# Dummy products, smaller first weight loads and later constants at the start of a two-block decoder kernel

## The reference

```python
def rms_norm(x, g):
    xf = x.astype(jnp.float32)
    y = xf * lax.rsqrt(jnp.mean(xf * xf, axis=-1, keepdims=True) + RMS_EPS)
    return (y * g.astype(jnp.float32)).astype(x.dtype)

def first_block(...):
    h = rms_norm(x, norm1_g[l])
    proj = h @ w_in[l]                     # 2048 wide, in blocks of 512 columns
    qa, ka, va, ra, ga, qb, kb, vb = jnp.split(proj, split_points, axis=-1)
...
    qb = rms_norm(qb.reshape(Bsz, S, DIL_HEADS, DIL_DH), q_norm_g[l])
    kb = rms_norm(kb.reshape(Bsz, S, DIL_HEADS, DIL_DH), k_norm_g[l])
...
    x = x + mix @ w_out[l]
    h2 = rms_norm(x, norm2_g[l])
    x = x + (jax.nn.silu(h2 @ w_gate[l]) * (h2 @ w_up[l])) @ w_down[l]
```

## Time and profile before

| | |
|---|---|
| time, median of 3 runs | 1984.41 us (1983.95 to 1984.6) |
| the profiled execution | 1984.17 us, of which 1982.4 are its span |
| TensorE busy | 1963.4 us (99%) |
| VectorE, ScalarE, GpSimd busy | 1098.0 us (55%), 940.4 us (47%), 108.1 us (5%) |
| DMA | 352.74 MB, mean 178 GB/s |

### The profile page before, as it was taken

One profiled execution on the slowest core, in us unless ns is written; L12 is line 12 of the kernel. 1 busy time (PEld: TensorE's weight loads), 2 busy tenths in 40 slices (PEclk: granted clock), 3 DMA queues, 4 the chain that ended last, 5 costly groups with the idle time before them and its releaser, 6 DMA issues.

```text
span 1982.4 us, 22700 instructions
## 1 busy us (share of the span) xinstructions
PE 1963.4 (99%) x9062; PEld 1609.4 (81%) x9062; DVE 1098.0 (55%) x1330; ACT 940.4 (47%) x1230; POOL 108.1 (5%) x326
## 2 busy tenths in 40 slices
PE   8999999999999999999999999999999999999998
PEld 6788887788888888888888888888888887777787
DVE  4556455664445544455445565545556566666664
ACT  5445454554444344443444554444444454655652
POOL 1111000200000000000000010001100011100000
PEclk9999999999999999999999999999999999999999
DMA  7566564566665666666666566665566655444445
GB/s 232 179 192 170 151 176 153 159 180 183 196 190 189 195 191 185 190 190 192 195 189 190 184 186 193 189 191 171 167 184 190 191 180 176 132 138 140 138 132 164
DMA packets 182441, 352.74 MB, mean 178 GB/s; under 512 B 11136, under 2 KB 11952, under 8 KB 182336
## 3 DMA queue, kind: packets, MB, share of 16 engines
q1 hardware_dynamic: 181520, 349.18, 58.6%
q0 software_dynamic: 816, 2.11, 0.7%
HBM read 349.14 MB, written 2.11 MB: 177 GB/s over the span
## 4 chain that ended last, share of the span: by engine, by line
PE 92%; DVE 2%; POOL 2%; issue 1%; ACT 1%; DMA 0%; SPq 0%; DVEq 0%; POOLq 0%; ACTq 0%
PE g L773 29%; PE g L775 28%; PE g L774 28%; PE m L738 3%; PE m L841 1%; DVE wl L1201 1%; PE m L840 1%; DVE TW L1201 1%; DVE st L1210 1%; POOL st L1565 1%; ACT TW L961 1%; PE m L847 1%; ACT wh L964 1%; POOL st L1563 0%; POOL st L1569 0%
## 5 line engine op out<-in xcount | busy, mean ns | idle before, releaser
L1201 DVE TENSOR_TENSOR wl<-raw,wh 128x1024 fp32r<-128x1024 f32 x657 | 801.4, 1223 | 772.3 <-ACT wh L964 772.1
L964 ACT ACTIVATE wh<-raw 128x1024 fp32r<-128x1024 f32 x657 | 694.7, 1059 | 853.1 <-PE g L775 850.0
L773 PE MATMUL g<-wh,xh 128*128 128x512 f32 x1888 | 749.5, 397 | 2.6 <-DVE wl L1201 2.6
L775 PE MATMUL g<-wh,xl 128*128 128x512 f32 x1888 | 737.1, 390 | 0.0
L774 PE MATMUL g<-wl,xh 128*128 128x512 f32 x1888 | 736.1, 390 | 0.0
L773 PEld LDWEIGHTS g<-wh,xh 128*128 128x128 f32 x1888 | 355.1, 188 | 82.7 <-issue 8.5
L775 PEld LDWEIGHTS g<-wh,xl 128*128 128x128 f32 x1888 | 354.9, 188 | 75.4
L774 PEld LDWEIGHTS g<-wl,xh 128*128 128x128 f32 x1888 | 355.4, 188 | 70.1
L773 PE MATMUL g<-wh,mh 128*128 128x512 f32 x736 | 291.8, 396 | 0.0
L775 PE MATMUL g<-wh,ml 128*128 128x512 f32 x736 | 287.1, 390 | 0.0
L774 PE MATMUL g<-wl,mh 128*128 128x512 f32 x736 | 286.9, 390 | 0.0
(11 more groups left out here) (127 smaller groups left out, 872.5 us busy)
## 6 DMA issues: line engine op xcount, KB each, us to landing
raw<-in_ev_w_in SPq DMA_DIRECT2D x128, 512.0 KB, 3.7
raw<-in_w_in SPq DMA_DIRECT2D x96, 512.0 KB, 3.9
raw<-in_w_gate SPq DMA_DIRECT2D x88, 512.0 KB, 4.4
raw<-in_w_up SPq DMA_DIRECT2D x88, 512.0 KB, 3.7
raw<-in_w_down SPq DMA_DIRECT2D x88, 512.0 KB, 3.8
raw<-in_od_w_in SPq DMA_DIRECT2D x72, 512.0 KB, 3.7
raw<-in_w_out SPq DMA_DIRECT2D x32, 512.0 KB, 3.9
raw<-in_ev_w_out SPq DMA_DIRECT2D x32, 512.0 KB, 4.8
```

The costliest lines, as they stand in the source:

```text
L773: e.matmul(o, hi[:, kt, c], h, start=first, stop=False)
L775: last = e.matmul(o, lo[:, kt, c], h, start=False, stop=end)
L964: return e.activation(o, i, AF.Copy, scale=scale)
L1201: return e.tensor_tensor(o, a, b, op)
```

## The change

Five things change. (1) The first block's first unit is cut in two units of one row block each, so the first two loads are of 256 KB and that block has nine units in place of eight; all later units have a number that is one higher. (2) These two loads are issued by ScalarE as its first instructions; SP issues the others, x parts 0 and 1 first. (3) A new step `warm`: VectorE fills 384 columns of TE with 0.5, and TensorE makes four float32 products of 256 columns from it, into a PSUM bank that is overwritten later. (4) The steps of the start stand in another order: `cut 0` before the first `xturn`, and all eight `xturn` before the first `sq`. (5) The small constants are loaded after the load of unit 12.

```diff
@@ all_units
-        for a in range(0, len(b.kts), per):
-            units.append(Unit(len(units), b, b.kts[a:a + per], a == 0, a + per >= len(b.kts)))
+        starts = [0, 1] if b.i == 0 else []
+        starts += range(per if starts else 0, len(b.kts), per)
+        for a, z in zip(starts, starts[1:] + [len(b.kts)]):
+            units.append(Unit(len(units), b, b.kts[a:z], a == 0, z == len(b.kts)))
@@ Plan.lay
         self.lanes["post"].append(self.first_acts())
+        say("warm")
+        say("cut", 0)
         self.step()
-        say("cut", 0)
         self.step()
         say("cut", 1)
...
-            if b.n == 512:
+            if len(un.kts) == 2:
                 say("mul", u, 1)
@@ Plan.first_acts
         for kt in range(0, KT, 2):
             self.say("xturn", "X0", kt)
-            if kt % 4 == 2:
-                self.say("sq", 0, kt // 4)
+            yield
+        for j in range(4):
+            self.say("sq", 0, j)
             yield
         self.say("norm", 0)
@@ tensor
+                elif kind == "warm":
+                    on.wait_ge(s_warm, 1)
+                    for i in range(4):
+                        e.matmul(MB[2][:, 0:256], TE[:, 0:128], TE[:, 128:384], start=True, stop=True)
@@ scalar
             te_free = (s_act_step, 0)
+            weights(e, 0).then_inc(s_raw[0], 16)
+            weights(e, 1).then_inc(s_raw[1], 16)
@@ vector
+                elif kind == "warm":
+                    e.memset(TE[:, 0:384], 0.5).then_inc(s_warm, 1)
@@ sync
             e.dma_start(small[:, 0:nid], t["small"][:, 0:nid]).then_inc(s_id, 16)
-            load_x(0)
-            load(0)
-            load_x(1)
-            load(1)
-            load_x(2)
-            e.dma_start(small[:, nid:], t["small"][:, nid:]).then_inc(s_small, 16)
+            tokens(e, 0).then_inc(s_x[0], 16)
+            tokens(e, 1).then_inc(s_x[1], 16)
             load(2)
-            load_x(3)
+            tokens(e, 2).then_inc(s_x[2], 16)
             load(3)
-            load_x(4)
+            tokens(e, 3).then_inc(s_x[3], 16)
             load(4)
+            tokens(e, 4).then_inc(s_x[4], 16)
             load(5)
...
                 if kind == "cut" and a[0] >= LEAD and a[0] + NR < N:
                     load(a[0] + NR)
+                    if a[0] == 8:
+                        e.dma_start(small[:, nid:], t["small"][:, nid:]).then_inc(s_small, 16)
```

More of the change, by code:

```diff
@@ L553, in program @@
         s_pv, s_ob_act, s_ob_dve = sem("s_pv"), sem("s_ob_act"), sem("s_ob_dve")
-        s_split = sem("s_split")
+        s_split, s_warm = sem("s_split"), sem("s_warm")
         s_sq, s_nsum = sem("s_sq"), sem("s_nsum")
@@ L731, in aw_free, with weights, tokens @@
             return full(*before[-1]) if before else (s_bank, 0)
+        def weights(e, u):
+            un = units[u]
+            b, m = un.block, len(un.kts)
+            w = t[b.w]
+            if b.col is None:
+                src = w.rearrange("p (t n) -> p t n", n=b.n)
+            else:
+                r0 = b.row + 128 * un.kts[0]
+                src = w[r0:r0 + 128 * m, b.col:b.col + b.n].rearrange("(t p) n -> p t n", p=128)
+            return e.dma_start(raw[:, u % NR, 0:m * b.n].rearrange("p (t n) -> p t n", t=m), src)
+        def tokens(e, i):
+            a, z = XPARTS[i]
+            return e.dma_start(x[:, :, a:z], t["x"].rearrange("(t p) d -> p t d", p=128)[:, :, a:z])
         def tensor(e):
@@ L739, in four @@
                 return last
-            on.wait_ge(s_id, 16)
             for p in plan.order:
@@ L775, in tensor @@
                             last = e.matmul(o, lo[:, kt, c], h, start=False, stop=end)
-                    if half == 1:
+                    if half == len(un.kts) - 1:
                         last.then_inc(s_mul, 1)
+                elif kind == "warm":
+                    on.wait_ge(s_warm, 1)
+                    for i in range(4):
+                        e.matmul(MB[2][:, 0:256], TE[:, 0:128], TE[:, 128:384], start=True, stop=True)
                 elif kind == "xturn":
@@ L780, in tensor @@
                     if stage == 0:
+                        on.wait_ge(s_id, 16)
                         on.wait_ge(s_x[[lo <= 128 * kt < hi for lo, hi in XPARTS].index(True)], 16)
@@ L1551, in gpsimd @@
             steps = Steps(s_pool_step)
-            done = (s_root, 0)
             def root(p, dst, src, n, width, from_, dst_free=()):
@@ L1626, in sync @@
             on = Once(e)
+            nid = COLS["n1"][1]
             def load(u):
[L1629 to L1636, removed]
                 if u >= NR:
                     on.wait_ge(s_lo, u - NR + 1)
[L1639 to L1647, removed]
-            e.dma_start(small[:, 0:nid], t["small"][:, 0:nid]).then_inc(s_id, 16)
-            load_x(0)
-            load(0)
-            load_x(1)
-            load(1)
-            load_x(2)
-            e.dma_start(small[:, nid:], t["small"][:, nid:]).then_inc(s_small, 16)
+                weights(e, u).then_inc(s_raw[u % NR], 16)
+            e.dma_start(small[:, 0:nid], t["small"][:, 0:nid]).then_inc(s_id, 16)
+            tokens(e, 0).then_inc(s_x[0], 16)
+            tokens(e, 1).then_inc(s_x[1], 16)
             load(2)
-            load_x(3)
+            tokens(e, 2).then_inc(s_x[2], 16)
             load(3)
-            load_x(4)
+            tokens(e, 3).then_inc(s_x[3], 16)
             load(4)
+            tokens(e, 4).then_inc(s_x[4], 16)
             load(5)
```

## The result

| | before | after |
|---|---|---|
| median of 20 runs | 1984.26 us (1983.07 to 1984.98) | 1987.51 us (1986.3 to 1988.4) |
| ratio | | 1.0017 (95% interval 1.0011 to 1.0023) |
| profiled execution | 1984.17 us, span 1982.4 | 1988.1 us, span 1986.3 |

The change made the kernel 3.25 us slower: under the 0.2% that was named as the bound of what can be told, but with an interval that doesn't hold 1. In effect no change was forecast (1984.9 us); the time lies at the very top of the range, a hundredth of a microsecond outside it. A few single executions took far longer than all others (7026.97 and 2173.36 us in e1, 4053.88 us in e4, 11331.34 us of the kernel before), and every median here leaves them out.

The account below looks back on a forecast made before the run. TensorE bounds the kernel, busy 1963.4 of 1982.4 us. A 2.8 us lead at the start, eaten by 2.8 us of later squares, plus 0.5 us for the bias step gives 1984.7, forecast as 1984.9 us; range 1983.1 to 1987.5.

Parts of the forecast that it names:

- Part 0 of x ... between the bounds 4.3 and 5.4 I take 4.9: At the start: the first x transfer lands at 4.9 us, between as if alone and one queue's curve by bytes.
- so I take the upper level from then on: At the start: TensorE, busy from 1.3 to 6 us, then runs at about 2.4 GHz, 0.23 us per product.
- Lead: ... 2.8 us: At the start: the unit of row blocks 2 and 3 starts at 11.9, before 14.25, with one transpose group more done.
- rival 1: At the start: upper clock level not reached by 7.7 us, costing 2.1 us, so 1987.0 us; chance 0.17.
- part 2 of x, taken at 9.4: At the start: this x transfer lands at 9.4 us, against 9.9 before, since two queues fill sooner.
- 8.58 us forecast: First norm: time from the end of the next-to-last unit to the evacuation, taken from 30.2 to 38.75.
- 2.97 for four squares: First norm: four pairs of squares on ScalarE behind the weight copy take 2.97 us (1.47 plus two times 0.75).
- all of GpSimd's steps near 0.19 us: First norm's root: no VectorE operation runs beside it, so the 1.22 us step shrinks, saving 1.03 us.
- The stall of near 4 us: Behind the first evacuation: TensorE waits near 4 us for its next weights, until 43.37, in place of 1.09.
- The bias addition taken at 0.5: Head norm: VectorE's addition now comes after the evacuation, on the chain to the transposes, adding 0.5 us.
- Rival 3: Behind the first norm: the stall drops TensorE to 1.2 GHz, costing 0.4 us (1985.3) or 2.8 us (1987.7); chance 0.10.
- the extra unit adds two short operations: First block: the added unit brings two short operations on engines with room, moving nothing.

Follow-up runs that it names:

- e1: The changed kernel with the squares and the norm back at their old places among the transposes: 1982.01 us, ratio 0.9987.
- e4: The changed kernel without the dummy products and VectorE's fill: 1988.03 us, ratio 1.0019.
- e10: The kernel before with its first two weight loads (512 KB each, uncut) issued by ScalarE, so asked for earlier: 1985.4 us, ratio 1.0008.
- e3: The changed kernel with the two small first weight loads issued by SyncE between the x parts again: 1985.69 us, ratio 1.0008.
- e5: The changed kernel with the squares at their old places and the first weights on SyncE's queue again: 1980.85 us, ratio 0.9982.
- e7: e5 with dummy products of 128 columns also in the two gaps of the start: 1980.69 us, ratio 0.9982.
- e8: The changed kernel with eight thrown-away float32 products of 256 columns in the 3.9 us stall behind the first norm: 1987.37 us, ratio 1.0012.
- e2: The kernel before with the squares and the norm moved behind all transposes, and nothing else: 1989.76 us, ratio 1.0027.
- e6: The kernel before with its first unit cut in two, and nothing else: 1983.11 us, ratio 0.9995.
- e11: e5 without the dummy products: 1980.9 us, ratio 0.9984.
- e12: e11 with the 697 KB of small constants loaded early, behind part 2 of x, as in the kernel before: 1981.66 us, ratio 0.9988.
- e9: e7 with part 2 of x asked for ahead of the third weight load: 1981.83 us, ratio 0.9990.

## Why the prediction was wrong

**The step that failed** is "Part 0 of x ... between the bounds 4.3 and 5.4 I take 4.9", with what hung on it: "so I take the upper level from then on", and the "Lead: ... 2.8 us". Part 0 landed at 5.9, outside the bounds. I had interpolated on the landing curve of one queue, by bytes. With the weights asked for on a second queue at the same moment it took 4.7 us from asking to landing, and 2.9 to 3.6 us in the traces with one queue; even the 72 KB identity went from 1.9 to 3.2 us. e10 shows the same by itself (4.8 us to landing, a first product 1.45 us later), e3 its removal, both with the earlier asking in it. The rule of the Trainium skill (DMA: Bandwidth & Descriptors, Queues, rings and completion order) that engines take turns between queues was the one to follow; e10 agrees with it, and its price was 1.0 us above the value that I took, not 0.5.

TensorE then had gaps of 0.9 and 1.1 us in its start, behind dummy products that ended at 5.1, and the pace stayed low until 14.2. That these gaps kept it low isn't shown: e5 kept the fast pace over a gap of 1.31 us, and e3 lost it after gaps of 0.7 and 1.0. The first weight product came at 9.00, not 7.7 (1.3 us), and from it to the unit of row blocks 2 and 3 went 6.0 us, not 4.2 (1.8 us). The lead of 2.8 us became a lag of 0.4. That is rival 1, priced at 2.1 us and given 0.17, and the late landing on top of it.

The lead of 2.8 us was too large even for an early x. It also hung on part 2 of x, taken at 9.4. It landed at 10.3 in the changed kernel, which the slow products hid, and near 10.5 and 11.1 in e7 and e5. In e7, with part 0 there in time and the pace of 0.23 from the first weight product on, the lead is 14.25 - 12.76 + 0.46 = 1.95 us; no run here had more. The dummy products took 3.8 us (1.33 to 5.11), where 3.4 were taken, and the wait for x hid that.

**What held.** The stall is the squares' and not the start's: it is 3.9 us in e3 too, and gone in e1. From the end of the next-to-last unit to the evacuation: 8.58 us forecast, 41.98 - 33.37 = 8.61 measured. In it, 2.97 for four squares (34.59 to 37.63 are 3.04) and all of GpSimd's steps near 0.19 us, as the Trainium skill's SBUF — State Buffer, Who interferes with whom, had it. The stall of near 4 us was 3.94. The bias addition taken at 0.5 was 0.54. Rival 3 came true in its short form, 0.4 us: the granted clock was 0.50 for 4.9 us behind the stall, and e8 measures 0.48.

**The sum again** with the measured lag: 1984.7 + 2.8 + 0.4 for the start + 0.4 for the clock = 1988.3 us, against 1988.1 of the profiled execution. The medians differ by less (3.25), since that execution was one of the slower of its kernel.

**What was right for less than it looked.** I had the moved squares eat the lead at one for one, 2.8 us. e1 and e2 show them to cost 5.5 to 5.6. The difference is a part of the change that I had put down as costing nothing, "the extra unit adds two short operations": with a ninth unit and the norm in its old place, the evacuation comes one unit later against the norm (3.0 us behind the unit ahead in e1, 5.75 before). Both are in the 8.58 us, so the sum was right, but as a ledger of the parts it was not. By parts, in the medians against the kernel before: squares +5.6 (e2), second queue +1.6 (e10), small units -1.5 (e6, whose interval holds no change); dummy products and late constants each between -1 and 0, not settled (e4, e5, e7, e11, e12). These sum to 3.7 to 5.7, and the whole is 3.25; they don't simply add, since small units take back part of what the squares cost.

**Open.** How far the 0.9 us of e3 that its trace puts on the pace would hold in other executions, since when the clock rises and falls differs between them (e5's first products had the fast pace, e3's did not); whether the weights on their own queue or their being asked for earlier delays x; and why part 2 of x came no earlier in e9. Late constants were tried only against e11.

## What to carry to other kernels

A transfer that the first instruction waits for should have nothing large asked for ahead of it or beside it: weights on a second queue at the same moment made part 0 of x 1.1 to 1.9 us later here. Work moved behind the last feeding step of a block delays the block's evacuation, and every load step behind the evacuation in that engine's list with it; look what stands last in the list ahead of the wait, not how busy the engine is. Dummy products can pay only where the faster first products would not have to wait for the next transfer: e11 reached the time of e5 without them, within noise, and the best kernels here (e5, e7, e11, near 1980.8 us, 3 to 4 us under the kernel before) share small first units, one queue, squares at their old places and late constants.

## What the runs showed of the hardware that I had not expected

- In e6 the clock was 0.66 on average from 17.5 to 22 us, behind a wait of 1.78 us. Behind the wait of 1.65 us in e5 the products kept the pace of 0.23, and behind the 1.09 us stall of the kernel before the first product took 0.50 us, against 0.79 at the low pace. In the changed kernel the clock was 0.78 on average already inside the 3.94 us stall.
- From 9 to 11 us the granted-clock column read 1.00 in the kernel before, the changed one, e4 and e11, where the pace was 0.43 us; behind the stall it read 0.50 for the same pace, and so it did in e3, from 7.8 to 11 us. A 1.00 at a program's start is to be held against the pace.
